# Third product ahead of the fourth in a seven-product block multiplication, with VectorE's reading order turned to match

## The reference

```python
h2 = _rmsnorm(x, g_fn)
gt, up = jnp.split(h2 @ w_fi, 2, axis=-1)      # w_fi: 1024 x 5632
x = x + (jax.nn.silu(gt) * up) @ w_fo          # w_fo: 2816 x 1024
...
y = _rmsnorm(x, g_final)
```

## Time and profile before

| what | us |
|---|---|
| median of 3 runs (981.93 to 981.97) | 981.95 |
| profiled execution | 981.5 |
| its span | 980.0 |
| PE busy | 937.4 (96%) |
| DVE busy | 779.6 (80%) |
| ACT busy | 465.7 (48%) |

### The profile page before, as it was taken

The page is one execution under the profiler, slowest core; times in us unless marked ns, Lnnn a source line. Parts: engine busy times, 40 slices in busy tenths (PEclk is TensorE's granted clock), DMA queues, the critical chain, the costliest instruction groups (busy, mean ns, idle before and its releaser), DMA issues. The chain is left out here.

```text
span 980.0 us, 18425 instructions
## 1 busy us (share of the span) xinstructions
PE 937.4 (96%) x6830; PEld 913.2 (93%) x6830; DVE 779.6 (80%) x1219; ACT 465.7 (48%) x679; POOL 123.2 (13%) x116
## 2 busy tenths in 40 slices
PE   5999989999999999999999999999999999999992
PEld 5999979999999999999999999999999999999892
DVE  6875778698779859796445569899888999899996
ACT  5643335346334524453833345355445554555562
POOL 4133042006002300510212000000000000000002
PEclk9988989999999999999999999999999999999997
DMA  6226511620451152124242222232222222322212
GB/s 188 87 65 146 93 44 55 236 86 22 160 173 65 45 223 86 43 96 131 89 159 87 81 69 87 87 118 96 89 86 88 86 95 81 127 87 86 87 44 96
DMA packets 25091, 97.26 MB, mean 99 GB/s; under 512 B 6816, under 2 KB 6960, under 8 KB 20672
## 3 DMA queue, kind: packets, MB, share of 16 engines
q1 hardware_dynamic: 23280, 78.01, 24.8%
q0 software_dynamic: 1744, 18.42, 6.1%
HBM read 84.03 MB, written 12.39 MB: 98 GB/s over the span
## 5 line engine op out<-in xcount | busy, mean ns | idle before, releaser
L1215 PE MATMUL ps<-h_hi,w_hi 128*128 128x288 f32 x896 | 194.3, 298 | 1.5 <-DVE w_lo L1586 1.5
L1215 PE MATMUL ps<-h_lo,w_hi 128*128 128x288 f32 x896 | 192.1, 296 | 0.0
L1215 PE MATMUL ps<-h_hi,w_lo 128*128 128x288 f32 x896 | 192.0, 296 | 0.0
L767 ACT ACTIVATE w_hi<-raw 128x1024 fp32r<-128x1024 f32 x76 | 80.3, 1057 | 188.5 <-PE ps L1215 175.7
L1215 PEld LDWEIGHTS ps<-h_hi,w_hi 128*128 128x128 f32 x896 | 143.6, 189 | 3.5 <-issue 2.8
L1215 PEld LDWEIGHTS ps<-h_hi,w_lo 128*128 128x128 f32 x896 | 144.8, 189 | 0.0
L1215 PEld LDWEIGHTS ps<-h_lo,w_hi 128*128 128x128 f32 x896 | 144.6, 189 | 0.0
L1586 DVE TENSOR_TENSOR w_lo<-raw,w_hi 128x1024 fp32r<-128x1024 f32 x76 | 95.3, 1254 | 59.9 <-ACT w_hi L767 59.7
L1801 DVE SCALAR_TENSOR_TENSOR conv<-a_p,vec,conv x120 | 96.9, 807 | 0.2
L1487 PE MATMUL ps<-cols_b,late 128*128 128x288 f32 x432 | 63.8, 296 | 4.9 <-ACT tmp L1065 4.5
L1487 PEld LDWEIGHTS ps<-cols_b,late 128*128 128x128 f32 x432 | 58.8, 188 | 6.6 <-issue 5.9
(11 more groups left out here) (338 smaller groups left out, 1888.5 us busy)
## 6 DMA issues: line engine op xcount, KB each, us to landing
raw<-w_head_in SPq DMA_DIRECT2D x40, 512.0 KB, 3.5
raw<-w_fp_in SPq DMA_DIRECT2D x18, 1024.0 KB, 4.9
cs<-st_c_in POOLq DMA_DIRECT2D x4, 2048.0 KB, 9.7
c_s_out<-cs POOLq DMA_DIRECT2D x4, 2048.0 KB, 7.7
raw<-w_fo_in SPq DMA_DIRECT2D x8, 1024.0 KB, 4.8
x<-xT_in SPq DMA_DIRECT2D x16, 288.0 KB, 4.3
raw<-w_cgcv_in SPq DMA_DIRECT2D x8, 512.0 KB, 3.6
raw<-w_ga_in SPq DMA_DIRECT2D x8, 512.0 KB, 3.6
```

The lines of the kernel that those rows point to most:

```text
L767: act.activation(w_hi[:, s, :], raw[:, s, :], ACT.Copy).then_inc(hi_ready, 1)
L1215: last = pe.matmul(ps[:, 2 * s + b, 0:HALF], wt[:, w, k * P:k * P + P], src[:, k, b * HALF:b * HALF + HALF], start=(k == 0 and wt is w_hi ...
```

## The change

TensorE does the third product of the round left over ahead of the fourth, except in round 26: the order of a round goes from P1(i), P4(i-1), P2(i), P3(i-1), P6(i), P5(i), P7(i) to P1(i), P3(i-1), P2(i), P4(i-1), P6(i), P5(i), P7(i), and the two products behind the last round change places as well. VectorE reads the fifth product of an out round at the start of the next round, ahead of `sums_1_3`, and adds the fourth last. `up_right` stays where it is.

```diff
@@ hi_a22_s4 (ScalarE)
                 if i:
                     act.wait_ge(p_done["P3"], i)
+                    act.wait_ge(p_done["P4"], i)
@@ TensorE
             for i in range(NR):
                 p1(i)
-                if i:
+                if i == OUT_AT[LAST_G]:
                     p4(i - 1)
-                if i == OUT_AT[LAST_G]:
                     p3(i - 1)
                     p5(i)
                     p2(i)
                     p6(i)
                 else:
+                    if i:
+                        p3(i - 1)
                     p2(i)
                     if i:
-                        p3(i - 1)
+                        p4(i - 1)
                     p6(i)
                     p5(i)
                 p7(i)
+            p3(NR - 1)
             p4(NR - 1)
-            p3(NR - 1)
@@ gated_tile (VectorE)
                 dve.wait_ge(mid_read, i + 1)
+                dve.wait_ge(p_done["P4"], i + 1)
@@ VectorE, readers of an out round
             def x_of_u3(i):
+                dve.wait_ge(mid_read, i + 1)
                 dve.wait_ge(snapped, 3 * i + 3)
...
             def x_of_p5(i):
-                x_wait(i, 1)
                 dve.wait_ge(p_done["P5"], i + 1)
...
@@ VectorE, the loop
+                if is_out(i - 1):
+                    x_of_p5(i - 1)
                 sums_1_3(i)
...
                 sum_4(i)
-                if is_out(i - 1):
-                    x_of_p5(i - 1)
...
                 lo_s2(i)
                 if is_out(i - 1):
-                    x_of_p4(i - 1)
+                    x_of_p1_u2(i - 1)
                 lo_s1_s3(i)
                 if is_out(i - 1):
-                    x_of_p1_u2(i - 1)
+                    x_of_p3(i - 1)
...
                 elif is_out(i - 1):
-                    x_of_p3(i - 1)
+                    x_of_p4(i - 1)
                     lo_a22_s4(i)
...
+            x_of_p5(NR - 1)
             x_of_u3(NR - 1)
-            x_of_p5(NR - 1)
-            x_of_p4(NR - 1)
             x_of_p1_u2(NR - 1)
             x_of_p3(NR - 1)
+            x_of_p4(NR - 1)
```

More of the change, by code:

```diff
@@ L2254, in x_of_p4 @@
                 dve.tensor_tensor(x_half(i, 1, 0), x_half(i, 1, 0), bank_of(i, 0), ALU.add).then_inc(x_step, 1)
+                x_wait(i, 4)
+                dve.wait_ge(mid_read, i + 1)
+                dve.sem_inc(set_free, 1)
+                dve.sem_inc(x_step, 1)
+                if ROUNDS[i][1] == LAST_G:
+                    dve.sem_inc(x_row, 2)
             def x_of_p1_u2(i):
@@ L2262, in x_of_p3 @@
             def x_of_p3(i):
-                x_wait(i, 3)
+                x_wait(i, 2)
                 dve.wait_ge(p_done["P3"], i + 1)
                 dve.tensor_tensor(x_half(i, 0, 1), x_half(i, 0, 1), bank_of(i, 2), ALU.subtract).then_inc(x_step, 1)
[L2266 to L2271, removed]
             def add_row_square(j):
```

## The result

| | before | after |
|---|---|---|
| median (us) | 981.96 of 4 runs (981.93 to 982.52) | 1011.78 of 4 runs (1011.19 to 1012.63) |
| ratio | | 1.0303 (95%: 1.029 to 1.0316) |
| profiled execution | 981.5 | 1012.63 |
| its span | 980.0 | 1011.1 |
| PE / DVE busy | 937.4 (96%) / 779.6 (80%) | 948.8 (94%) / 785.3 (78%) |

The kernel is 29.8 us slower. The forecast was 1002.7 with a range up to 1009, so the sign was right and the size 9 us short. The mean granted clock of TensorE was 0.975 to 0.977 in the four executions, and 0.984 in the profiled one of the kernel before. In the changed file the lines are one to three higher: `up_right` is L2114, `sums_1_3` L2063, the product's matmul L1488.

What follows compares the result with a forecast made beforehand. TensorE was busy 96%, pulled behind VectorE's full work list in heavy rounds. Three runs' lags, 6.97 + 7.23 + 6.82, less 0.29 at the end, gave +20.7 on 981.5; with 0.45 for the median, 1002.7 us, range 997 to 1009.

Steps and rivals of the forecast that it cites:

- What the change moves: In rounds: `snap_u3` waits (5.1 us) go; P3 waits for `up_right` instead, some 17 times, 23 to 27 us.
- The loop: `up_right` to next `up_right` via P3, P2, P4, P6, silu, gated tile: 12.04 us light (first-half tile), 13.37 heavy (second-half).
- The hand-over of 0.51 us: In rounds: P3 starts 0.51 us after `up_right` starts, taken from the row of round 26.
- Out rounds: Reading the fifth product early fills idle VectorE time and nothing waits: cost and gain 0.
- The end: Behind the last round, P3 goes first instead of P4 waiting for the copy of P7: gain 0.29 us.
- The product's 1.59 us: Time per TensorE product, four times in each loop: 132.5 ns per matmul from the rows, against the skill's 122.5.
- TensorE's clock falls: Rival: waits of about 2 us halve the clock for 5 us in 10 heavy loops, +25 us, 1028; chance 0.05.
- The loop stays open: Rival: P3 waits but VectorE still sets the pace, heavy 11.98 us, light 11.52; 986; chance 0.05.
- Faster: Rival: `snap_u3` waits of 5.1 us go and `up_right` hides behind P1; 976.5; chance 0.02.
- it does not do what it says: Rival: P3 and P4 wait for the same event, so nothing changes; 982; chance 0.02.

Runs made afterwards that it cites:

- The filled kernels: Changed kernel plus extra matmuls nobody reads ahead of P3 in nine rounds with 2 us waits: eight matmuls, median 1005.14 us; four, 1000.47 us.

## Why the prediction was right and wrong

- **What the change moves: right.** The waits for `snap_u3` went, P3's wait for `up_right` came, 18 times and 23.7 us (said: some 17, and 23 to 27), 0.68 us in a light round behind a light one and 2.01 in a heavy one.
- **The loop: right.** 13.40 and 12.07 us for 13.37 and 12.04, each event on its path within 0.03. The hand-over of 0.51 us and the wait of P3, both from one row of round 26, carried over to 17 other rounds. The filled kernels, where nothing else disturbs, give 296.31 and 296.42 for a stretch worked out as 295.99.
- **Out rounds: right as far as shown.** Cost 0, and the interval of the kernel with only these reordered holds that of no change; the late load of round 18 is the open end. **The end** gained 0.59 - 0.35 = 0.24 us behind the last P7, for 0.29.
- **The product's 1.59 us: right.** Four products of the loop take 6.45 us, and the rule of the Trainium skill ("TensorE: Matmul & The Clock Gate", Back-to-back issue gap), which by the prediction's estimate would have made the stretch 7 us shorter, does not hold for this stream: from P2's start to P4's its 12 matmuls take 657.17 - 655.59 = 1.58 us, 132 ns each.
- **The step that failed is the rival *TensorE's clock falls*.** It was taken as all or nothing: 2.5 us on each of 10 heavy loops, with a chance of 0.05, and left out of the range. It came true in part: 4 of the 9 waits of 2 us, 1.5 us on each, 6.0 us (3 of them in each of two other profiles). The prediction set a fall behind 4.41 us against none behind 0.62. That left 2 us open, and with it the number of loops hit, from 0 to 10. Half of them at 2.5 us would have given 1015, and the range should have gone so far. The size per loop was also too high: the lower clock lasted some 3 us and not 5. And the prediction's "one wait of 4.41 us" passes over rows of the same trace in which the clock fell behind less, here after small products and a wait of 0.80 us:

```profile
69.30 0.85 PE L1215 MATMUL ps<-xg_hi,w_hi 128*128 128x288 f32 x2 [0.80 <-DVE w_lo L1586]
```

```profile
65.00:70.00 5.00, 4.20 (x38) 3.62 (x38) 3.97 (x5) 1.63 (x2) 1.75 (x2) 0.86 0.01 2
70.00:75.00 5.00, 5.00 (x23) 5.00 (x23) 3.48 (x5) 1.37 (x2) 2.79 (x2) 0.50 0.32 108
```

  So the length of a wait alone did not tell whether the clock would fall, and a chance of 0.05 had these rows against it.
- **The range had no room for the rest of the span.** It was made from bounds of the loop alone. The rest gave +1.62 ahead of the rounds, +0.72 for one load and +1.05 for the last mean. The first and the last differed between profiles of kernels that are alike there, so they are scatter; for the load that is not settled. One profiled execution does not show how wide such scatter is.
- **The other rivals.** *The loop stays open* would have shown heavy rounds of 11.98 us; they were 13.40. *Faster* needed P3's wait to vanish, and *it does not do what it says* needed the old waits; neither row is there.

Slower was forecast with 0.96 and came. Had the clock stayed up, the same profile would have ended at 1012.63 - 6.0 = 1006.6, inside the range.

## What to carry to other kernels

Where an engine's wait is moved into a path that comes back to itself, write down the loop event by event; its length times the number of rounds was right here to 0.03 us a round. Before a product is moved ahead, ask what its releaser stands behind on its own engine: one VectorE sum of 1.1 us in front of `up_right` accounted for 22 of the 28 us, 6 of them through the clock. And when a change makes TensorE idle for longer in each round than the profile has shown to be harmless, price the clock per round, with a number of rounds hit between none and all, and put it into the range.

## What the runs showed of the hardware

- Idle times of TensorE of 2.0 us were at times followed by a granted clock of 0.50, 1.2 GHz, for some 3 us, while it had been at 1.00 for hundreds of us: 10 of the 27 waits of 2.00 to 2.15 us in three profiles (4, 3 and 3 of 9). Each cost 1.5 us. Which ones changed from execution to execution. In the same rounds it was not seen behind idle times of 1.5 us (9 waits) and about 1 us (9 waits). Elsewhere it fell behind less, as at 69 us of the trace of before, after small products and a wait of 0.80 us. The Trainium skill ("TensorE: Matmul & The Clock Gate", What's actually happening) says that the throttled state is the default and activity releases it; the fall behind idle time agrees.
- The 12 matmuls from P3's start to P2's take 3.05 us where the clock fell early in them, 254 ns each, against 141 where it did not (1.69 us, the first behind a wait among them).
- Filling idle time with matmuls whose result nobody reads made the kernel faster: 12 us between the medians on one chip for four of them in nine rounds, of which 5.2 us lie in the rounds by the profiles; the rest lies ahead of them and is not shown to come from the filling.
